# Delta-rule recurrence: state update issued ahead of the outputs; 64-wide block products; last output tile split in two

## The reference, cut to what matters

```python
def step(S, inp):
    r_t, w_t, k_t, v_t, kk_t, a_t = inp
    sa = jnp.einsum('bhvk,bhk->bhv', S, -kk_t)
    S = (S * w_t[:, :, None, :]
         + sa[..., None] * (kk_t * a_t)[:, :, None, :]
         + v_t[..., None] * k_t[:, :, None, :])
    y_t = jnp.einsum('bhvk,bhk->bhv', S, r_t)
    return S, y_t
...
_, y = lax.scan(step, S0, (tm(r_h), tm(decay_h), tm(k_h), tm(v_h), tm(kk), tm(a_h)))
```

## Time and profile before

| | us |
|---|---|
| three runs, median (lowest to highest) | 768.8 (766.02 to 770.76) |
| the profiled execution, its own time | 772.9 |
| its span | 771.1 |
| TensorE matmul busy | 730.7 (95%) |
| VectorE busy | 448.3 (58%) |
| ScalarE busy | 305.8 (40%) |
| GpSimd busy | 172.3 (22%) |

### The profile page before, as it was taken

One profiled execution on the slowest core, in us unless ns is written; L12 is line 12 of the kernel. 1 busy time (PEld: TensorE's weight loads), 2 busy tenths in 40 slices (PEclk: granted clock), 3 DMA queues, 4 the chain that ended last, 5 costly groups with the idle time before them and its releaser, 6 DMA issues.

```text
span 771.1 us, 17652 instructions
## 1 busy us (share of the span) xinstructions
PE 730.7 (95%) x7606; PEld 595.6 (77%) x7606; DVE 448.3 (58%) x803; ACT 305.8 (40%) x649; POOL 172.3 (22%) x132
## 2 busy tenths in 40 slices
PE   5999999999999978977799999999999999999997
PEld 4588788777788767767788888877777777776897
DVE  5864633777999433356754414769645666754711
ACT  5644443565633112333442456333234353424300
POOL 2244330000134322324311001920000000004651
PEclk9999999999989989999999999999999999999999
DMA  8123225223165863560006037022301111133131
GB/s 259 56 83 109 64 74 164 82 83 81 45 151 124 177 221 119 177 205 5 4 3 219 1 110 173 11 85 81 108 27 55 55 56 45 40 103 103 56 110 55
DMA packets 116765, 72.83 MB, mean 94 GB/s; under 512 B 26832, under 2 KB 114128, under 8 KB 116688
## 3 DMA queue, kind: packets, MB, share of 16 engines
q1 hardware_dynamic: 98496, 65.12, 28.6%
q10 hardware_dynamic: 18192, 6.58, 3.5%
HBM read 64.35 MB, written 7.34 MB: 93 GB/s over the span
## 4 chain that ended last, share of the span: by engine, by line
PE 85%; DVE 7%; issue 3%; ACT 2%; DMA 1%; POOL 1%; POOLq 0%; ACTq 0%; DVEq 0%
PE bank L537 19%; PE bank L1019 9%; PE bank L531 7%; PE bank L533 7%; PE bank L532 7%; PE bank L1060 2%; PE bank L1043 2%; PE bank L658 2%; DVE arena L1637 2%; PE bank L797 2%; PE bank L1153 2%; PE bank L1155 1%; PE bank L1154 1%; PE bank L690 1%; PE bank L1033 1%
## 5 line engine op out<-in xcount | busy, mean ns | idle before, releaser
L537 PE MATMUL bank<-arena 128*128 128x256 f32 x736 | 165.0, 381 | 0.0
L537 PEld LDWEIGHTS bank<-arena 128*128 128x128 f32 x736 | 137.9, 190 | 24.9 <-issue 7.0
L2085 POOL TENSOR_TENSOR w_lo<-arena,w_hi 128x1024 fp32r<-128x1024 f32 x24 | 59.4, 2474 | 179.8 <-ACT w_hi L1265 179.8
L1265 ACT ACTIVATE w_hi<-arena 128x1024 fp32r<-128x1024 f32 x44 | 46.4, 1057 | 79.8 <-DMA arena<-w_in 78.4
L531 PE MATMUL bank<-x_hi,w_hi 128*128 128x512 f32 x192 | 77.4, 403 | 0.4 <-POOL w_lo L2085 0.4
L533 PE MATMUL bank<-x_hi,w_lo 128*128 128x512 f32 x192 | 76.2, 397 | 0.0
L532 PE MATMUL bank<-x_lo,w_hi 128*128 128x512 f32 x192 | 76.2, 397 | 0.0
L531 PEld LDWEIGHTS bank<-x_hi,w_hi 128*128 128x128 f32 x192 | 36.6, 191 | 9.9 <-issue 1.2
L2181 POOL COPY arena<-arena 128x512 f32<-128x512 f32 x4 | 2.5, 616 | 186.8 <-DVE arena L1992 186.8
L533 PEld LDWEIGHTS bank<-x_hi,w_lo 128*128 128x128 f32 x192 | 36.5, 190 | 8.5
L532 PEld LDWEIGHTS bank<-x_lo,w_hi 128*128 128x128 f32 x192 | 36.6, 191 | 8.0
(11 more groups left out here) (265 smaller groups left out, 1597.2 us busy)
## 6 DMA issues: line engine op xcount, KB each, us to landing
arena<-w_in SPq DMA_DIRECT2D x45, 512.0 KB, 3.8
arena<-w_ada SPq DMA_DIRECT2D x12, 1024.0 KB, 6.4
arena<-w_in SPq DMA_DIRECT2D x8, 1024.0 KB, 5.4
arena<-w_out SPq DMA_DIRECT2D x8, 1024.0 KB, 5.4
lt_dram<-arena ACTq DMA_DIRECT2D x16, 256.0 KB, 2.3
arena<-x SPq DMA_DIRECT2D x4, 512.0 KB, 5.3
arena<-x SPq DMA_DIRECT2D x1, 2048.0 KB, 7.8
out<-arena SPq DMA_DIRECT2D x8, 256.0 KB, 2.1
```

The source lines that it names most:

```text
L537: last = mm(o, lhs(k), rhs(k), start=(k == 0), stop=(k == n - 1))
L1265: A(WHI[n % 3][:, :], WR[n % 3][:, 0:1024], ACT.Copy).then_inc(weights_rounded, 1)
L2085: TT(WLO[n % 3][:, :], WR[n % 3][:, 0:1024], WHI[n % 3][:, :].bitcast(f32), SUB)\
```

## The change

Four edits. (1) `scan_out`: the eight calls for `s_out` come ahead of the eight for `y_out`; GpSimd's `values_beside` waits for `y_made` of group `g-2` where it waited for `s_made`, since `y` is now the last reader of `SAV`. (2) `first_l`: eight products of 64 x 64 for each head, one per chunk, in place of four of 128 x 128; a chunk with odd `e` is written to partitions 64 to 127 of the bank. (3) The last output tile `("z", 3, 1)` becomes two, `("z", 3, 2)` and `("z", 3, 3)`, each in a bank of its own with 256 columns. VectorE multiplies each, GpSimd adds the residual to the first and VectorE to the second. (4) The last store becomes two of 128 KB, with the semaphore `last_ready` for the second.

```diff
@@ first_l
-                for j in range(NT):
-                    at = slice(j * P, (j + 1) * P)
+                for e in range(NE):
+                    at = slice(e * CH, (e + 1) * CH)
                     for h in range(2):
-                        last = mm(o[h][:, at], AB[side[h], c, at], AR[side[h], 0, c, at], start=True, stop=True,
+                        last = mm(o[h][side[e % 2], at], AB[side[h], c, at], AR[side[h], 0, c, at], start=True, stop=True,
                                   skip_group_check=True)
@@ scan_out
-                if e == 0:
-                    pe.wait_ge(y_copied, g)
-                for i in range(4):
-                    for h in range(2):
-                        last = mm(y_out[side[h], i, :], GMG[g][:, h, i, CH:P], SAV[:, g % 2, i, h, :],
-                                  start=(e == 0 and i == 0), stop=True, skip_group_check=True)
-                last.then_inc(y_made, 1)
                 if e < NE - 1:
...
                     last.then_inc(s_made, 1)
+                if e == 0:
+                    pe.wait_ge(y_copied, g)
+                for i in range(4):
+                    for h in range(2):
+                        last = mm(y_out[side[h], i, :], GMG[g][:, h, i, CH:P], SAV[:, g % 2, i, h, :],
+                                  start=(e == 0 and i == 0), stop=True, skip_group_check=True)
+                last.then_inc(y_made, 1)
@@ last product, TensorE
-                    o = next_bank(("z", nb, th))
+                    ends = (nb, th) == (3, 1)
+                    o = next_bank(("z", nb, 2 if ends else th))
                     for i in range(2):
+                        if ends and i:
+                            o = next_bank(("z", nb, 3))
...
-                    full(last, ("z", nb, th))
+                        if ends:
+                            full(last, ("z", nb, 2 + i))
+                    if not ends:
+                        full(last, ("z", nb, th))
@@ SyncE
+            for i in range(2):
+                sp.wait_ge((out_ready, last_ready)[i], (8, 1)[i])
+                sp.dma_start(out_t[:, 2 + i, 768:1024], OUTB[3][:, i, :]).then_inc(out_stored[3], 16)
@@ VectorE
+            dve.wait_ge(out_stored[3], 16)
+            for i in range(2):
+                key = ("z", 3, 2 + i)
+                o = OUTB[3][:, i, :]
+                free(TT(o, arrived(dve, key)[:, i * 256:(i + 1) * 256], GX[:, 768:1024], MUL), key)
+            stored(dve, ("z", 3, 3))
+            TT(o, o, X1[:, 3, 768:1024], ADD).then_inc(last_ready, 1)
@@ GpSimd, values_beside
                 if g >= 2:
-                    pool.wait_ge(s_made, g - 1)
+                    pool.wait_ge(y_made, g - 1)
@@ GpSimd, the end
-                TT(OUTB[i % 4], OUTB[i % 4], X1[:, 2 * th:2 * th + 2, at], ADD).then_inc(out_ready, 1)
+                if i < 7:
...
+                else:
+                    stored(pool, ("z", nb, 2))
+                    TT(OUTB[3][:, 0, :], OUTB[3][:, 0, :], X1[:, 2, at], ADD).then_inc(out_ready, 1)
```

More of the change, by code:

```diff
@@ L383, in rwkv_then_grid_block @@
         qk_squared, qk_done = sem("qk_squared"), sem("qk_done")
-        gate2_tanh, bm_ready, masked, out_ready, folded, sines_out = [
-            sem(n) for n in ("gate2_tanh", "bm_ready", "masked", "out_ready", "folded", "sines_out")]
+        gate2_tanh, bm_ready, masked, out_ready, last_ready, folded, sines_out = [
+            sem(n) for n in ("gate2_tanh", "bm_ready", "masked", "out_ready", "last_ready", "folded", "sines_out")]
         def cols(w, a, n):
@@ L615, in first_l @@
                 o = [next_bank(("lt", c, h)) for h in range(2)]
-                for j in range(NT):
-                    at = slice(j * P, (j + 1) * P)
+                for e in range(NE):
+                    at = slice(e * CH, (e + 1) * CH)
                     for h in range(2):
-                        last = mm(o[h][:, at], AB[side[h], c, at], AR[side[h], 0, c, at], start=True, stop=True,
+                        last = mm(o[h][side[e % 2], at], AB[side[h], c, at], AR[side[h], 0, c, at], start=True, stop=True,
                                   skip_group_check=True)
-                        if j == NT - 1:
+                        if e == NE - 1:
                             last.then_inc(bank_full[where["lt", c, h][0]], 1)
@@ L1226, in _ @@
                         sp.dma_start(REL[cl * GH:(cl + 1) * GH, :], src).then_inc(rel_here, 16)
-            for i in range(8):
+            out_t = out.rearrange("(t p) n -> p t n", p=P)
+            for i in range(7):
                 nb, th = divmod(i, 2)
                 sp.wait_ge(out_ready, i + 1)
[L1230 to L1233, removed]
+                sp.dma_start(out_t[:, 2 * th:2 * th + 2, 256 * nb:256 * nb + 256], OUTB[i % 4])\
+                    .then_inc(out_stored[i % 4], 16)
+            for i in range(2):
+                sp.wait_ge((out_ready, last_ready)[i], (8, 1)[i])
+                sp.dma_start(out_t[:, 2 + i, 768:1024], OUTB[3][:, i, :]).then_inc(out_stored[3], 16)
+            for i, s in enumerate(out_stored):
+                sp.wait_ge(s, 48 if i == 3 else 32)
         @block.scalar
@@ L2194, in _ @@
                     split_w2(3)
-                stored(pool, ("z", nb, th))
                 at = slice(nb * 256, (nb + 1) * 256)
-                TT(OUTB[i % 4], OUTB[i % 4], X1[:, 2 * th:2 * th + 2, at], ADD).then_inc(out_ready, 1)
+                if i < 7:
+                    stored(pool, ("z", nb, th))
+                    TT(OUTB[i % 4], OUTB[i % 4], X1[:, 2 * th:2 * th + 2, at], ADD).then_inc(out_ready, 1)
+                else:
+                    stored(pool, ("z", nb, 2))
+                    TT(OUTB[3][:, 0, :], OUTB[3][:, 0, :], X1[:, 2, at], ADD).then_inc(out_ready, 1)
 _OUT = (1, T, D)
```

## The result

The changed kernel takes 765.3 us (median of 13 runs, 762.1 to 766.7) where the kernel before takes 768.7 in the 13 runs beside it (765.5 to 771.3). The ratio is 0.995 with a 95% interval of 0.9935 to 0.9964: 3.8 us less, between 2.8 and 5.0. A second measurement on another chip gave 0.994 (0.9914 to 0.9966). The interval separates the improvement from nothing, and it is smaller than the 1% that the prediction took as the least a measurement can tell.

What follows compares the result with a forecast made beforehand. TensorE was taken as the bound, busy 95% of the span, with waits for instruction packets as its second limit in the recurrence. Terms 2.5 + 1.5 + 1.2 = 5.2 us took 768.8 to 763.6; range 758.0 to 769.0.

Steps and rivals of the forecast that it cites:

- Block products: `first_l` stage: each block 0.50 us shorter; blocks 0 to 3 give 2.0 us, block 7 gives 0.50; 2.5 us in all.
- What is on the path there: Block-product stage: TensorE bounds blocks 0 to 3 and 7; blocks 4 to 6 only lengthen its wait before `bonus(7)`.
- Stage one gives nothing: Rival, block-product stage: the DRAM trip, not TensorE, sets 188 to 211 us, taking back 2.5 us; 766.1 us, chance 0.14.
- Order in `scan_out`: Recurrence: `s_out` ahead of `y_out` cuts state waits by 2.0 of 3.1 us; 1.5 us after packets, bounds 0.5 and 2.1.
- The quarter that was taken off for packets: Recurrence: waits for TensorE's instruction packets take back a quarter of the `scan_out` gain, 2.0 us becoming 1.5.
- The small stalls: Recurrence: a new issue stall near 286 to 296 us if instruction packets take the `scan_out` gain.
- Tail: After TensorE's last product: split multiply and add end 1.15 us sooner, last store 0.05 sooner; 1.2 us, bounds 0.9 and 1.5.
- The places of later packet ends move little.: Recurrence: the 256 records and weight loads added by block products, about one instruction packet, move later packet ends little.
- the long stall: At 273.5 us an instruction packet is 3.88 us late behind 355 GB/s of transfers; TensorE then runs at half clock.
- The slower rival: Recurrence: the same transfer burst catches a second packet, costing 3.9 us of stall and 3.4 of half clock; 770.9, chance 0.06.
- the first rival: Recurrence, 273.5 us: the late packet's stall and half clock go, saving 7.3 us more, 12.5 in all; 756.3, chance 0.10.

Runs made afterwards that it cites:

- `blocks_only`: Only the edit of `first_l` (block products by chunks) made to the kernel before; ratio 0.998, some 1.5 us less.
- `hold_loads`: Changed kernel with the second and third load of `w_ada` held until ScalarE has copied the first right side; ratio 0.9943 against the kernel before.

## Why the prediction was right

The forecast was 763.6 us with 758.0 to 769.0; measured were 765.3 in one set and 766.3 in the other. The sum was 5.2 us, the measurement 3.8 and 4.6. By its steps:

- **Block products, 2.5 predicted; 1.5 measured alone (-0.1 to 3.1).** This is the mis-sized term. The pace of the records was right (0.477 us for 32). Nothing was added for the change of the array's tile size, with the argument that L673 runs up to a full-array product at 355.21 and so has it included. That reading was wrong, and the trace of the kernel before had the price. A piece of the chain runs from the end of one record to the end of another, and 355.21 is where the last L673 ends. Start to start, from its timeline:

```profile
354.53 0.68 PE L673 MATMUL bank<-arena 64*64 64x64 f32 x32
355.14 0.66 PE L824 MATMUL bank<-arena 128*128 128x128 f32 x4
```

  That is 0.61 us, and the last L673 begins 0.15 before L824. The block took 0.62, with 0.147. So 0.12 is missing on the block, and 0.11 on L627: 0.27 per pass and 1.1 for four passes instead of 2.0. The Trainium skill's rule ("TensorEngine Tiling (Array Packing)", Key Properties), that a change of tiling mode drains TensorE, was cited against the edit and should have had a price; the trace agrees with it, by 0.147 us from the last record to the next weight load. Block 7 took 0.95 less instead of 0.50 in the first profiles, where it ran wholly at half clock, and together with `bonus(7)` 0.46 less where both kernels compared ran at full clock.
- **What is on the path there.** The chain leaves TensorE for the blocks' trip through DRAM at 184.72 as it did at 188.04, and TensorE's wait at `bonus(7)` grew to 2.30 (2.7 said, from 3 x 0.5; from 3 x 0.27 it would be 2.0). The 3.3 us between the two starts are the 2.2 that lie ahead of every edit and the 1.1 of four passes. "Stage one gives nothing" isn't excluded by the time of `blocks_only`, whose interval ends at 1.0001, but by the traces: `bonus(7)` starts 1.1 us sooner in all four kernels with the edit, counted from the same product.
- **Order in `scan_out`, 1.5 predicted, 1.5 measured alone (-0.4 to 3.2).** The wait went from 3.1 to 1.0, as worked out. The small stalls came where they were said, though two of the three are also in one of the four profiles without the edit. The quarter that was taken off for packets was a guess, and no run measures it: 1.5 lies in the middle of a wide interval.
- **Tail, 1.2 predicted, 1.45 in every profile and 1.7 measured alone (0.0 to 3.5).** The 1.15 of VectorE and GpSimd came out exactly. The store of half the size was taken at 0.05 sooner and was 0.3 sooner, its upper bound.
- **The total.** It came out near because the shortfall of the first term (2.5 for 1.6 by the traces at equal clock) was met in part by the tail (1.45 for 1.2), and the second term's size is known only within its interval. The range was wide enough for either measurement.
- **"The places of later packet ends move little."** Right, and it carried more than the sentence showed. The edit adds exactly 256 instructions: the long stall stands behind 3687 weight loads and matmuls before and 3943 after. The prediction counted "about one packet" and named no price for a number that isn't one. With half a packet more it cost 11.7 us, more than twice the whole gain. The slower rival named the right mechanism (a packet caught by the burst) with a price of 7.3 us, but as the point from which it decides it had TensorE's distance from the burst, where the runs show the count of instructions modulo 256.
- **The long stall** stayed, as most of the chance had it. That it can shrink without a gain (`hold_loads`: 3.88 to 1.14, the same time) says the first rival's 7.3 us was priced as if nothing would take its place.

## What to carry to other kernels

Price a change of TensorE's tile size where blocks are split into smaller ones: the records may go at twice the pace, and here 0.11 to 0.15 us stayed at each change of size. The rows of another place in the same kernel that changes size can hold the price, read from start to start and not from the chain's pieces. Where small products follow each other so fast that packets of instructions set the pace, compare variants only with the same number of TensorE instructions ahead of the dense part (modulo 256), or test an added quarter and half packet by itself: otherwise an edit is judged by where it put the packet ends. Two profiles of the same kernel can differ by as much as the edit is worth, here 3.2 and 3.7 us, so read stages and not spans. A stage counted from one product to another in every trace at hand separated 1.1 us where the time of the whole kernel could not.

## What the runs showed that was not expected

- 128 further instructions, whose work fits into a wait, moved the kernel by 1.5%, and 256 by nothing. In all fourteen kernels' traces the stalls of the recurrence sit at 193 or 194 modulo 256 (own count of TensorE's matmuls, weight loads and semaphore instructions).
- One quarter of a packet cost 10 us, most of it in time at half clock: 30.7 us of the recurrence for 17.1.
- The way from 64 x 64 to 64-row, 128-column tiles costs 0.147 us between the last record and the next weight load, and the way in 0.05 us more on the first four records than on any later four. From 64 x 64 to the full array it is 0.15 (L673 to L824).
- A last store of 128 KB ended the span 0.3 us sooner than one of 256 KB: 2.31 to 2.34 us from issue to the span's end in ten traces for 2.61 to 2.64 in four.
- Keeping one packet (269.6) clearer of the burst left the next one (274.7) late, and the half clock came behind that one.
